# Two modulation blocks multiplied during the router's choice, and the expert buffers in another order

## The chip, the cores and the metric

The kernel runs on one core of one Trainium2 chip. The metric is the device time of one execution in microseconds. All the weights come from the chip's memory in each execution.

## What is computed

Two transformer blocks stand one behind the other, for 256 tokens of width 1024. The change lies in the first one. Cut to what matters:

```
mod = silu(c) @ w_ada + b_ada                 # 1 x 6144: six rows of 1024
sh_m, sc_m, gt_m, sh_f, sc_f, gt_f = split(mod, 6)
h = modulate(rmsnorm(x, g), sh_m, sc_m)
mix = concat(forgetting_attention(h), multiscale_pool(h)) @ w_out
x = x + gt_m * mix
h = modulate(rmsnorm(x, g2), sh_f, sc_f)
lg, le = h @ w_rg + b_rg, h @ w_re + b_re     # router: 4 groups, 8 experts in each
# the best group, in it the best two experts, weights from two softmaxes
y = sum over 32 experts of weight * (silu(h @ w_gate) * (h @ w_up)) @ w_down
x = x + gt_f * y
```

The product for `mod` is made in 12 blocks of 512 columns. Blocks ten and eleven are `gt_f`, the gate by which the experts' sum is multiplied at the end of the block. Nothing before the experts' results needs them. The second block (`second_block` in the reference) has a projection to 5632 columns, two kinds of attention, and an MLP of width 4096.

## The kernel before

**Weights as pieces.** All large weights arrive as pieces of 128 x 2048 numbers (1 MB). SyncE issues them in one fixed order: a list `pieces`, whose entry `i` goes into buffer `ring[slot[i]]`. One transfer is one instruction on SyncE's queue, and SyncE waits and issues strictly in order. Before each issue it waits until the piece that was in the buffer before has been used (`freed`). The first 36 pieces are the weights up to the end of the first block's mixer; the last four of them are the two halves each of modulation blocks ten and eleven. Then come 96 expert pieces from number `E0` on, and from `E1` on the weights of the second block. The experts are worked on in groups of four (`y`): four gate-and-up pieces of the first half, four of the second, and the four down pieces, which come behind the gate-and-up pieces of the next group.

**The buffers of the expert pieces.** Seven are the ring's own (`NR = 7`, `raw0` to `raw6`). The others become free as the mixer ends: `XP` is the memory of x, `GP` that of the gathered tokens, `YP` that of the tile `ym`; eight more are the split weights `whi0`, `wlo0` to `whi3`, `wlo3` (each is the memory of a buffer with a number of 7 or more), and two (`HL`, `HL + 1`) the split activations. `turns` is the order in which the expert pieces take these buffers round by round, `first` the order of the first round, with `GP` and `YP` in it, and `ends` that of the last pieces. `last` holds the seven ring buffers in the order in which the mixer's pieces leave them: `last[0:3]` held block nine's halves and a piece of w_out, `last[3:7]` the four pieces of blocks ten and eleven. In the list before, `first` is XP, GP, last[0:5], whi0, wlo0, last[5:7], whi1, wlo1, YP, whi2, wlo2, whi3, wlo3, HL, HL + 1.

For the three borrowed buffers and the split ones the issuing function `sp_piece` waits for the end of the work that used them:

```
if slot[i] == XP:
    e.wait_ge(*at(("x0", "turned", 3)))
elif slot[i] == GP:
    e.wait_ge(*at(("valued", 3)))
elif slot[i] == YP:
    for n in (("valued", 3), ("mixed", 3), ("ada_rows", 11)):
        e.wait_ge(*at(n))
elif slot[i] >= NR:
    e.wait_ge(*at(("wread", 8 + (slot[i] - NR) % NS if slot[i] < HL else 11)))
```

`wread 8` and `wread 9` come with the first and the second half of the first round of products with w_out (`pe_mix_part(e, n, 1)`, n below 4 and from 4 on), `wread 10` and `wread 11` with those of the second round. `("ada_rows", b)` comes with the last of block b's products. These read `crep`, the activated vector c repeated to 32 columns, and `crep` lies inside the memory that later is `ym`.

**A modulation block.** `pe_block` multiplies its two pieces by `crep` in 8 matmuls of 32 columns of weights and 512 numbers of output (`pe_rows`). ScalarE copies the partial rows to `acc` (`act_ada`). For blocks ten and eleven `pe_ada` adds the partial rows by one more product, and VectorE adds the result to `GTF` (`dve_ada`). Every product here is in full fp32 except those of the split weights; a matmul in fp32 shows in the trace as two instructions.

**The order of the work.** TensorE: first round with w_out for n below 4, block ten, the router's constant row (`shift`), block eleven, first round for n from 4 on, the second round with w_out (n from 0 to 7) with the closing products of both blocks behind n = 1 and the transposes back and the router's logits between; then `pe_moe`. This begins with five dummy products (`pe_awake`), waits for `mask`, makes the rank products (each chosen token's place in its expert), one more dummy, and then gathers the tokens and runs the expert groups. VectorE makes the router's choice meanwhile (`dve_route`), the picking matrices (`dve_pick`), the low halves of the normalised rows (`dve_low_rows`) and the weights. `Banks([...])` gives out banks of PSUM in turn; taking one waits until what was in it has been read.

Of the kernel before, what the change touches and what calls it, by code (L numbers as in the profile page):

```python
# [107 lines left out]
def build(nc, a, out):  # L108
# [3 lines left out]
    with root:  # L112
# [228 lines left out]
        for i in range(NP):  # L341
            if i == E0:
                last = [(taken + k) % NR for k in range(NR)]
                parts_ = [NR + k + NS * h for k in range(NS) for h in range(2)]
                turns = [XP] + last[0:5] + parts_[0:2] + last[5:] + parts_[2:] + [HL, HL + 1]
                first = turns[0:1] + [GP] + turns[1:12] + [YP] + turns[12:]
                ends = [NR, NR + NS] + parts_[2:6] + [(E1 + k) % NR for k in range(NR)] + parts_[6:] + [HL, HL + 1, XP]
            if pieces[i][0] == "exp":
                n = i - E0 - len(first)
                k = first[n] if n < 0 else turns[n % len(turns)] if i < E1 - len(ends) else ends[i - E1 + len(ends)]  # L350
                last_exp[k] = i
            elif i in fixed:
                k = fixed[i]
            else:
                k = (taken if i < E0 else i) % NR
                taken += 1
            earlier.append(in_slot.get(k))
            use.append(1 + slot.count(k))
            slot.append(k)
            in_slot[k] = i  # L360
# [139 lines left out]
        def act_ada(e, b):  # L500
            e.wait_ge(*at(("ada_rows", b)))
            e.wait_ge(*at(("mod", b - 2)))
            e.activation(acc[b % 2][:, :], bank(("ada_rows", b))[:, :], ACT.Copy).then_inc(
                *ada_act(("read", ("ada_rows", b)), ("acc", b)))
# [62 lines left out]
        def dve_ada(e, b):  # L567
            if 6 <= b < 10:
                s = dve_turn_back(e, acc[b % 2], ("ada_rows", b))
                e.tensor_tensor(mcol[:, b // 2, 4 * (b % 2):4 * (b % 2) + 4], s, badc[:, 4 * b:4 * b + 4], ALU.add).then_inc(  # L570
                    *mix_dve(("mod", b)))
                return
            p = bank(("ada", b))
            e.wait_ge(*at(("ada_sum", b)))
            if b >= 10:
                d = GTF[:, 512 * (b % 2):512 * (b % 2) + 512]
                e.wait_ge(*loaded("gtf"))
                e.tensor_tensor(d, d, p[:, :], ALU.add).then_inc(*mix_dve(("read", ("ada", b)), ("mod", b)))
            else:
                d = mcol[:, b // 2, 4 * (b % 2):4 * (b % 2) + 4]  # L580
                e.wait_ge(*loaded("badc"))
                e.tensor_tensor(d, p[:, 0:4], badc[:, 4 * b:4 * b + 4], ALU.add).then_inc(
                    *mix_dve(("read", ("ada", b)), ("mod", b)))
# [189 lines left out]
        def act_mixer(e):  # L773
            e.preload_act_table_set("natural_log_exp_and_others")
            e.wait_ge(*loaded("c"))
            e.activation(ce[:, :], cc[:, :], ACT.Exp, scale=-1.0).then_inc(*mix_act("ce"))
            for t in range(2):
                if t == 0:
                    e.wait_ge(*loaded("first"))
                act_stat(e, t, loaded("x"), mix_act, "n1")  # L780
            act_pieces(e, 3)
            act_high(e, mix_act, "n1", (0,))
            act_pieces(e, 5)
            act_high(e, mix_act, "n1", (1,))
            act_pieces(e, 10)
            act_high(e, mix_act, "n1", (2,))
            act_pieces(e, 13)
            act_high(e, mix_act, "n1", (3,))
            act_pieces(e, 14)
            e.wait_ge(*at("flog_parts"))  # L790
            e.activation(dT[:, 0, :], bank("flog_parts")[:, 0:256], ACT.Copy).then_inc(*mix_act(("read", "flog_parts"), "flog_out"))
            act_copy(e, qT, -0.125, mix_act, "q")
            act_pieces(e, 16)
            e.wait_ge(*at("lt"))
            e.activation(lf[:, :, :], lt[:, :, :], ACT.Abs).then_inc(*mix_act())
            e.wait_ge(*mix_act.last())
            e.activation(lf[:, :, :], lf[:, :, :], ACT.Exp, scale=-1.0).then_inc(*mix_act())
            e.wait_ge(*mix_act.last())
            e.activation(lf[:, :, :], lf[:, :, :], ACT.Ln, bias=1.0).then_inc(*mix_act("lf_log"))
            act_copy(e, kT, 1.0, mix_act, "k")  # L800
            act_pieces(e, 18)
            act_rows(e, vt, 0, mix_act, "v")
            act_soft(e, 0)
            act_soft(e, 1)
            act_rows(e, vt, 1, mix_act, "v")
            act_pieces(e, 21)
            act_soft(e, 2)
            act_soft(e, 3)
            act_rows(e, ut, 0, mix_act, "u")
            act_xt(e, range(2))  # L810
            act_pieces(e, 23)
            act_xt(e, range(2, 4))
            act_soft(e, 4)
            act_soft(e, 5)
            act_rows(e, ut, 1, mix_act, "u")
            act_heads(e, 0)
            act_soft(e, 6)
            act_soft(e, 7)
            act_heads(e, 1)
            for g in range(2):  # L820
                act_band(e, g)
            act_pieces(e, 29)
            for g in range(2, 4):
                act_band(e, g)
            act_heads(e, 2)
            for g in range(2):
                act_pooled(e, g)
            for g in range(2, 4):
                act_pooled(e, g)
            act_pieces(e, 31)  # L830
            act_heads(e, 3)
            act_ada(e, 10)
            act_ada(e, 11)
            act_pieces(e, E0)

        def act_soft(e, h):
# [30 lines left out]
        def dve_mixer(e):  # L867
# [106 lines left out]
            for n in range(8):  # L974
                e.wait_ge(*at(("mix_sum", n)))
                e.wait_ge(*at(("x0", "T", n // 2)))
                e.scalar_tensor_tensor(out=XT[:, n, :], in0=ps[n % 4][:, 256 * (n // 4):256 * (n // 4) + 256],
                                       scalar=mcol[:, 2, n:n + 1], in1=XT[:, n, :], op0=ALU.mult, op1=ALU.add).then_inc(
                    *mix_dve(("x1", n), ("read", ("x1", n))))
                if n == 1:  # L980
                    dve_ada(e, 10)
                    dve_ada(e, 11)

        def dve_scores(e, h):
            p = bank(("sc", h))
# [31 lines left out]
        def pe_mixer(e):  # L1017
# [87 lines left out]
            for n in range(4):  # L1105
                pe_mix_part(e, n, 1)
            rest = Banks([4, 5, 6])
            pe_block(e, rest, 10)
            p = rest.take(e, "shift")
            e.wait_ge(*at(("mod", 7)))  # L1110
            e.wait_ge(*loaded("wr"))
            for c in range(8):
                i = mm(e, p[:, 0:36], BF[:, c:c + 1].broadcast_to([128, 128]), WR[:, c, :], c == 0, c == 7)
            i.then_inc(*mix_pe("shifted"))
            pe_block(e, rest, 11)
            for n in range(4, 8):
                pe_mix_part(e, n, 1)
            for n in range(8):
                pe_mix_part(e, n, 0)
                if n == 1:  # L1120
                    for b in (10, 11):
                        pe_ada(e, Banks([5 + 2 * (b % 2)]), b)
                if n:
                    pe_back(e, n - 1)
                if n == 6:
                    pe_logits(e, 0)
                    pe_logits(e, 1)
# [8 lines left out]
        def pe_block(e, banks, b):  # L1136
            for k in range(2):
                pe_rows(e, banks, b, k)
# [108 lines left out]
        def act_moe(e):  # L1247
# [10 lines left out]
            for h in range(2):  # L1258
                for t in range(2):
                    e.activation(XNH[:, t, 512 * h:512 * h + 512], ps[4 + 2 * t + h][:, :], ACT.Copy, scale=rs[:, t:t + 1]).then_inc(  # L1260
                        *moe_act(("xnh", 2 * t + h)))
            e.wait_ge(*at("lg_less"))
            e.activation(r4[1][:, :, :], r4[1][:, :, :], ACT.Exp).then_inc(*moe_act("lg_exp"))
            for q in range(2):
# [36 lines left out]
        def dve_moe(e):  # L1301
            e.wait_ge(*at(("n2sq", 1)))
            e.tensor_tensor(ss[:, :], ss[:, :], ss2[:, :], ALU.add).then_inc(*rt_dve("ss"))
            dve_route(e)
            dve_pick(e, 0)
            dve_distance(e)
            dve_low_rows(e, 1)
            dve_flag(e)
            dve_weights(e)
            dve_spread(e, 0)  # L1310
# [159 lines left out]
            e.tensor_tensor(OH[0][:, :, :], OH[0][:, :, :], OH[1][:, :, :], ALU.add).then_inc(*step("weights"))  # L1470

        def pe_moe(e, banks):
            pe_awake(e, 5, ("x1", 5))
            p = Banks([3]).take(e, "rank")
            e.wait_ge(*at("mask"))
            mm(e, p[:, 0:32], C["su"], MK[:, 0, :], True, True)
# [1 line left out]
            mm(e, p[:, 32:64], C["su"], MK[:, 1, :], False, True)  # L1478
            mm(e, p[:, 64:96], C["ones"], MK[:, 0, :], True, False)
            mm(e, p[:, 64:96], C["ones"], MK[:, 1, :], False, True).then_inc(*moe_pe("ranked"))  # L1480
            pe_awake(e, 1, ("x1", 5))
            gb, ub, db, tb = Banks([0, 2]), Banks([1]), Banks([2, 0]), Banks([3])
            for q in range(2):
                pe_gather(e, gb, 0, q)
            for y in range(NQ + 1):
# [57 lines left out]
                           ring[slot[i[s]]][:, w], f == 0, f == 1)  # L1543
            x.then_inc(*moe_pe(("down", y, n), *[("freed", i[s]) for s in range(4)] if n else []))


        def pe_awake(e, n, before):
            e.wait_ge(*at(("read", before)))
            e.wait_ge(*loaded("later"))
            for i in range(n):  # L1550
                mm(e, ps[1][:, :], C["ident"], cst[:, NCONST - 512:], True, True)

        def pe_combine(e, y, n):
            e.wait_ge(*at(("WT", y)))
# [1077 lines left out]
```

## Time and profile before

| | us |
|---|---|
| median of 3 runs | 758.48 |
| lowest and highest | 758.19, 758.9 |
| span of the profiled execution | 756.9 |
| TensorE busy in it | 685.3 |
| VectorE busy | 366.3 |
| ScalarE busy | 291.0 |

The profiled execution's own time is its span, from the first instruction to the last. It lies 1.6 us under the median of the runs, which also holds what stands before the first and behind the last instruction. Shares of the whole span say little here, since the kernel has parts with different limits; the rows below are taken from stretches of it. A transfer's row gives when SyncE issued it; its landing is told in a row of its own as the time from the issue.

### The profile page before, as it was taken

The numbers are of one execution on the slowest core, as the hardware profiler recorded it, in microseconds if no ns is written. First come the engines' busy times: TensorE is split into PE (matmuls) and PEld (weight loads), VectorE is DVE, ScalarE is ACT, GpSimd is POOL, SyncE is SP. The second block draws the span as 40 slices with busy tenths as digits, with TensorE's granted clock in tenths as the row PEclk, the third lists the DMA queues.
The fourth block names the chain that finished last, engine by engine and source line by source line (L and its number), as shares of the span: only waits on it lengthen the run. The fifth ranks groups of instructions, "written<-read, shape, count | busy, mean of one in ns | idle before, by whom it ended". The sixth has DMA issues, their size and how long they took to land.

```text
span 756.9 us, 13008 instructions
## 1 busy us (share of the span) xinstructions
PE 685.3 (91%) x5450; PEld 534.3 (71%) x5450; DVE 366.3 (48%) x585; ACT 291.0 (38%) x426; POOL 48.7 (6%) x84
## 2 busy tenths in 40 slices
PE   3999999999767577768999999999999999999996
PEld 2987878843323132213999989999989999998895
DVE  3668861521101010104877987644875744555553
ACT  4345440341110010004666552668456543344532
POOL 0000000000000000000048650000000000000000
PEclk9999999999989898889999999999999999999999
DMA  8999999999999999999944534420655545664001
GB/s 352 405 415 409 358 421 419 421 419 422 424 422 423 424 422 425 397 417 417 374 180 158 215 119 171 159 111 1 223 175 187 197 145 215 223 220 170 1 1 55
DMA packets 33038, 210.27 MB, mean 278 GB/s; under 512 B 4688, under 2 KB 5072, under 8 KB 8656
## 3 DMA queue, kind: packets, MB, share of 16 engines
q1 hardware_dynamic: 32976, 209.38, 69.2%
q8 instruction: 46, 0.75, 0.4%
q14 instruction: 16, 0.13, 0.0%
HBM read 208.32 MB, written 1.05 MB: 277 GB/s over the span
## 4 chain that ended last, share of the span: by engine, by line
PE 71%; DMA 22%; DVE 2%; ACT 2%; SPq 1%; issue 1%; DVEq 0%
PE psum L421 70%; DMA raw<-in_w_exp 17%; DMA raw<-in_w_in_t 3%; PE psum L429 1%; SPq L476 1%; DMA raw<-in_w_in 1%; DMA raw<-in_w_ada_q 1%; ACT whi L497 0%; DVE X L2481 0%; DVE wlo L514 0%; ACT G L1293 0%; ACT XT L2428 0%; DVE gates L2090 0%; DVE dT L1012 0%; ACT MH L1859 0%
## 5 line engine op out<-in xcount | busy, mean ns | idle before, releaser
L421 PE MATMUL psum<-XH,whi 128*128 128x256 f32 x736 | 210.6, 286 | 3.8 <-DVE XL L667 2.5
L421 PE MATMUL psum<-XH,wlo 128*128 128x256 f32 x736 | 208.1, 283 | 0.0
L421 PE MATMUL psum<-XL,whi 128*128 128x256 f32 x736 | 207.8, 282 | 0.0
L514 DVE TENSOR_TENSOR wlo<-raw,whi 128x2048 fp32r<-128x2048 f32 (+1 forms) x88 | 168.7, 1957 | 35.8 <-ACT whi L497 35.8
L497 ACT ACTIVATE whi<-raw 128x2048 fp32r<-128x2048 f32 (+1 forms) x79 | 139.4, 1802 | 55.3 <-PE psum L421 37.1
L421 PEld LDWEIGHTS psum<-XH,whi 128*128 128x128 f32 x736 | 139.0, 189 | 8.5 <-issue 4.0
L421 PEld LDWEIGHTS psum<-XL,whi 128*128 128x128 f32 x736 | 138.7, 188 | 0.3
L421 PEld LDWEIGHTS psum<-XH,wlo 128*128 128x128 f32 x736 | 138.7, 189 | 0.0
L421 PE MATMUL psum<-raw,G 128*32 128x512 f32 x456 | 67.9, 684 | 20.0 <-DMA raw<-in_w_exp 20.0
L421 PEld LDWEIGHTS psum<-raw,G 128*32 128x32 f32 x456 | 17.9, 123 | 57.5 <-issue 56.5
L421 PE MATMUL psum<-raw,XT 128*32 128x512 f32 x248 | 38.0, 749 | 19.7 <-DMA raw<-in_w_exp 18.4
L1277 ACT ACTIVATE WT<-psum 128x256 f32<-128x256 f32 x8 | 3.1, 384 | 133.5 <-PE psum L421 97.6
L421 PE MATMUL psum<-whi,FL 128*128 128x512 f32 (+1 forms) x132 | 50.6, 384 | 0.0
L421 PE MATMUL psum<-wlo,FH 128*128 128x512 f32 (+1 forms) x132 | 50.6, 383 | 0.0
L421 PE MATMUL psum<-whi,FH 128*128 128x512 f32 (+1 forms) x132 | 50.5, 383 | 0.0
L421 PEld LDWEIGHTS psum<-raw,XT 128*32 128x32 f32 x248 | 10.1, 133 | 42.8 <-issue 42.8
L1341 DVE TENSOR_TENSOR ym<-psum,GT 128x512 f32<-128x512 f32 x16 | 11.1, 691 | 59.9 <-PE psum L421 59.9
L1331 DVE TENSOR_TENSOR XT<-XT,psum 128x256 f32<-128x256 f32 x8 | 3.4, 421 | 68.6 <-ACT XT L1282 68.6
L1744 POOL TENSOR_TENSOR XT<-xn 128x128 f32<-128x128 f32 x12 | 9.2, 767 | 392.6 <-DVE xn L2005 389.0
L421 PE MATMUL psum<-ym,WT 128*128 128x512 f32 x64 | 29.1, 595 | 0.9 <-DVE ym L1341 0.9
L2448 DVE TENSOR_TENSOR af<-af,psum 128x512 f32<-128x512 f32 x16 | 11.0, 686 | 38.9 <-ACT af L2407 38.9
L2407 ACT ACTIVATE af<-psum 128x512 f32<-128x512 f32 x16 | 9.6, 600 | 50.1 <-PE psum L421 50.0
(351 smaller groups left out, 947.3 us busy)
## 6 DMA issues: line engine op xcount, KB each, us to landing
raw<-in_w_exp SPq DMA_DIRECT2D x85, 1024.0 KB, 22.9
raw<-in_w_ff SPq DMA_DIRECT2D x32, 1024.0 KB, 5.3
raw<-in_w_in SPq DMA_DIRECT2D x22, 1024.0 KB, 7.3
raw<-in_w_ada SPq DMA_DIRECT2D x16, 1024.0 KB, 11.9
raw<-in_w_in_t SPq DMA_DIRECT2D x8, 1024.0 KB, 18.1
X<-in_w_exp SPq DMA_DIRECT2D x5, 1024.0 KB, 26.5
raw<-in_w_ada_q SPq DMA_DIRECT2D x4, 1024.0 KB, 17.3
raw<-in_w_out_t SPq DMA_DIRECT2D x4, 1024.0 KB, 12.3
```

The source lines that it names most:

```text
L421: return e.matmul(o, l, r, start=start, stop=stop, skip_group_check=True)
L429: return e.transpose(o, x, C["ident"][0:p, 0:p])
L476: e.dma_start(dst, src).then_inc(small[name], 16)
L497: e.activation(whi[j % NS][:, x], ring[slot[i]][:, x], ACT.Copy).then_inc(*hi_made(("hi", j), ("hi", j, x.start // 1024)))
L514: e.tensor_tensor(wlo[j % NS][:, x], ring[slot[i]][:, x], whi[j % NS][:, x], ALU.subtract).then_inc(*steps_(("lo", j, x.start // 1024), *[ ...
L1277: e.activation(WT[y % 2][:, :], bank(("w", y))[:, 0:256], ACT.Copy).then_inc(*moe_act(("read", ("w", y)), ("WT", y)))
L1331: e.tensor_tensor(ac[b], sa[b], bank(("gu", y))[:, 256:512], ALU.mult).then_inc(*moe_dve(("read", ("gu", y)), ("act", y)))
L1341: e.tensor_tensor(ym[:, y % 2, cs], bank(("d", y, n))[:, :], GTF[:, cs], ALU.mult).then_inc(*moe_dve(("read", ("d", y, n)), ("y", y, n)))
L1744: e.tensor_tensor(ev[:, :, 1, :], bv[:, :, 1, :], ref, ALU.subtract).then_inc(*hyb_pool())
L2407: e.activation(af[q][:, :], bank((("ff1", j), q))[:, :], ACT.Relu).then_inc(*ff_act(("relu", j, q)))
L2448: e.tensor_tensor(af[q][:, :], af[q][:, :], bank((("ff1", j), q))[:, :], ALU.mult).then_inc(*ff_dve(("read", (("ff1", j), q)), ("square", ...
```

## The change

Blocks ten and eleven are taken out of the mixer: their products (`pe_block`), their copies (`act_ada`), their closing products (`pe_ada`) and their additions (`dve_ada`). They now stand in the expert part. TensorE does both blocks and their closing products at the start of `pe_moe`, in place of the dummy products, ahead of the rank products. ScalarE's copies follow the first and the second half of XNH. VectorE's additions stand behind `dve_pick(e, 0)` and behind `dve_low_rows(e, 1)`. The gathers take banks 2 and 0 in that order.

The list of the expert buffers changes with it. `first` is now XP, GP, last[0:3], whi0, wlo0, whi1, wlo1, YP, whi2, wlo2, whi3, wlo3, HL, HL + 1, last[3:7]. The condition of `YP` in `sp_piece` is unchanged.

```diff
--- before.py
+++ after.py
@@ -342,8 +342,8 @@
             if i == E0:
                 last = [(taken + k) % NR for k in range(NR)]
                 parts_ = [NR + k + NS * h for k in range(NS) for h in range(2)]
-                turns = [XP] + last[0:5] + parts_[0:2] + last[5:] + parts_[2:] + [HL, HL + 1]
-                first = turns[0:1] + [GP] + turns[1:12] + [YP] + turns[12:]
+                turns = [XP] + last[0:3] + parts_ + [HL, HL + 1] + last[3:]
+                first = turns[0:1] + [GP] + turns[1:8] + [YP] + turns[8:]
                 ends = [NR, NR + NS] + parts_[2:6] + [(E1 + k) % NR for k in range(NR)] + parts_[6:] + [HL, HL + 1, XP]
             if pieces[i][0] == "exp":
                 n = i - E0 - len(first)
@@ -829,8 +829,6 @@
                 act_pooled(e, g)
             act_pieces(e, 31)
             act_heads(e, 3)
-            act_ada(e, 10)
-            act_ada(e, 11)
             act_pieces(e, E0)
 
         def act_soft(e, h):
@@ -977,9 +975,6 @@
                 e.scalar_tensor_tensor(out=XT[:, n, :], in0=ps[n % 4][:, 256 * (n // 4):256 * (n // 4) + 256],
                                        scalar=mcol[:, 2, n:n + 1], in1=XT[:, n, :], op0=ALU.mult, op1=ALU.add).then_inc(
                     *mix_dve(("x1", n), ("read", ("x1", n))))
-                if n == 1:
-                    dve_ada(e, 10)
-                    dve_ada(e, 11)
 
         def dve_scores(e, h):
             p = bank(("sc", h))
@@ -1105,21 +1100,16 @@
             for n in range(4):
                 pe_mix_part(e, n, 1)
             rest = Banks([4, 5, 6])
-            pe_block(e, rest, 10)
             p = rest.take(e, "shift")
             e.wait_ge(*at(("mod", 7)))
             e.wait_ge(*loaded("wr"))
             for c in range(8):
                 i = mm(e, p[:, 0:36], BF[:, c:c + 1].broadcast_to([128, 128]), WR[:, c, :], c == 0, c == 7)
             i.then_inc(*mix_pe("shifted"))
-            pe_block(e, rest, 11)
             for n in range(4, 8):
                 pe_mix_part(e, n, 1)
             for n in range(8):
                 pe_mix_part(e, n, 0)
-                if n == 1:
-                    for b in (10, 11):
-                        pe_ada(e, Banks([5 + 2 * (b % 2)]), b)
                 if n:
                     pe_back(e, n - 1)
                 if n == 6:
@@ -1259,6 +1249,7 @@
                 for t in range(2):
                     e.activation(XNH[:, t, 512 * h:512 * h + 512], ps[4 + 2 * t + h][:, :], ACT.Copy, scale=rs[:, t:t + 1]).then_inc(
                         *moe_act(("xnh", 2 * t + h)))
+                act_ada(e, 10 + h)
             e.wait_ge(*at("lg_less"))
             e.activation(r4[1][:, :, :], r4[1][:, :, :], ACT.Exp).then_inc(*moe_act("lg_exp"))
             for q in range(2):
@@ -1303,8 +1294,10 @@
             e.tensor_tensor(ss[:, :], ss[:, :], ss2[:, :], ALU.add).then_inc(*rt_dve("ss"))
             dve_route(e)
             dve_pick(e, 0)
+            dve_ada(e, 11)
             dve_distance(e)
             dve_low_rows(e, 1)
+            dve_ada(e, 10)
             dve_flag(e)
             dve_weights(e)
             dve_spread(e, 0)
@@ -1470,7 +1463,10 @@
             e.tensor_tensor(OH[0][:, :, :], OH[0][:, :, :], OH[1][:, :, :], ALU.add).then_inc(*step("weights"))
 
         def pe_moe(e, banks):
-            pe_awake(e, 5, ("x1", 5))
+            pe_block(e, Banks([1]), 10)
+            pe_block(e, Banks([2]), 11)
+            pe_ada(e, Banks([1]), 10)
+            pe_ada(e, Banks([0]), 11)
             p = Banks([3]).take(e, "rank")
             e.wait_ge(*at("mask"))
             mm(e, p[:, 0:32], C["su"], MK[:, 0, :], True, True)
@@ -1478,8 +1474,7 @@
             mm(e, p[:, 32:64], C["su"], MK[:, 1, :], False, True)
             mm(e, p[:, 64:96], C["ones"], MK[:, 0, :], True, False)
             mm(e, p[:, 64:96], C["ones"], MK[:, 1, :], False, True).then_inc(*moe_pe("ranked"))
-            pe_awake(e, 1, ("x1", 5))
-            gb, ub, db, tb = Banks([0, 2]), Banks([1]), Banks([2, 0]), Banks([3])
+            gb, ub, db, tb = Banks([2, 0]), Banks([1]), Banks([2, 0]), Banks([3])
             for q in range(2):
                 pe_gather(e, gb, 0, q)
             for y in range(NQ + 1):
@@ -1543,12 +1538,6 @@
                            ring[slot[i[s]]][:, w], f == 0, f == 1)
             x.then_inc(*moe_pe(("down", y, n), *[("freed", i[s]) for s in range(4)] if n else []))
 
-
-        def pe_awake(e, n, before):
-            e.wait_ge(*at(("read", before)))
-            e.wait_ge(*loaded("later"))
-            for i in range(n):
-                mm(e, ps[1][:, :], C["ident"], cst[:, NCONST - 512:], True, True)
 
         def pe_combine(e, y, n):
             e.wait_ge(*at(("WT", y)))
```

## Rows read from the trace of the kernel before

**Rows 1.** The page of the profile: its first line

```profile
span 756.9 us, 13008 instructions
```

**Rows 2.** Stretches: us, busy us (instructions) of each engine, granted clock, DMA share, GB/s

```profile
120.00:150.00 30.00, 29.78 (x212) 25.33 (x211) 11.71 (x41) 5.55 (x15) 0.00 (x0) 1.00 1.01 421
...
220.00:340.00 120.00, 84.60 (x472) 28.56 (x472) 11.21 (x21) 6.65 (x15) 0.00 (x0) 0.83 1.01 418
...
360.00:756.00 396.00, 389.47 (x3088) 358.60 (x3086) 248.23 (x317) 205.15 (x254) 48.56 (x80) 1.00 0.42 157
```

**Rows 3.** TensorE's waits from 150 to 360 us: in total, times, longest

```profile
PE psum L421 <- DMA raw<-in_w_exp: 42.8, 12, 6.3
```

**Rows 4.** Chain of work that ended last, 310 to 440 us: start, us, what

```profile
344.17 9.39 DMA raw<-in_w_in
...
356.86 3.08 PE psum L421 x24
```

**Rows 5.** Timeline of SyncE's issues from 115.5 us: start, us, line, transfer, number

```profile
115.84 7.53 SPq L461 DMA_DIRECT2D raw<-in_w_exp  x4
123.50 0.35 SPq L461 DMA_DIRECT2D ym<-in_w_exp  x1
130.90 10.18 SPq L461 DMA_DIRECT2D raw<-in_w_exp  x6
147.01 0.33 SPq L476 DMA_DIRECT2D GT<-in_norm_final_g  x1
155.64 0.33 SPq L461 DMA_DIRECT2D X<-in_w_exp  x1
```

**Rows 6.** Us to landing of the issues at 115.8, 155.6, 452.6, 454.8, 588.6, 590.8 us

```profile
raw<-in_w_exp SPq DMA_DIRECT2D x1, 1024.0 KB, 17.8
...
X<-in_w_exp SPq DMA_DIRECT2D x1, 1024.0 KB, 6.4
...
raw<-in_w_o_hg SPq DMA_DIRECT2D x1, 1024.0 KB, 4.9
...
raw<-in_w_o_sb SPq DMA_DIRECT2D x1, 1024.0 KB, 6.6
...
raw<-in_w_ff SPq DMA_DIRECT2D x1, 1024.0 KB, 4.8
...
raw<-in_w_ff SPq DMA_DIRECT2D x1, 1024.0 KB, 5.1
```

**Rows 7.** Timeline, 110.8 to 127 us: start, us, engine, line, operation [idle before]

```profile
110.96 1.92 PE L421 MATMUL psum<-raw,crep 128*32 128x512 f32 x16
112.81 1.97 PE L421 MATMUL psum<-GT,mcol 128*128 128x36 f32 x16
...
112.95 0.60 ACT L503 ACTIVATE acc<-psum 128x512 f32<-128x512 f32 x1 [5.26 <-PE psum L421]
...
114.72 1.93 PE L421 MATMUL psum<-raw,crep 128*32 128x512 f32 x16
...
125.22 1.88 PE L421 MATMUL psum<-acc,cst 128*128 128x512 f32 x4
126.94 0.27 PE L421 MATMUL psum<-cst,XT 128*128 128x128 f32 x1
```

**Rows 8.** Timeline of TensorE: dummies, rank products, gate and up of group 2

```profile
142.60 4.54 PE L421 MATMUL psum<-cst 128*128 128x512 f32 x10
...
147.13 1.27 PE L421 MATMUL psum<-MK,cst 128*128 128x32 f32 x10
...
177.94 0.59 PE L421 MATMUL psum<-X,G 128*32 128x512 f32 x1
```

**Rows 9.** Timelines of ScalarE and VectorE: XNH, mask, one addition to GT

```profile
143.16 2.43 ACT L1260 ACTIVATE XNH<-psum,rs 128x512 fp32r<-128x512 f32 x4
...
146.75 0.23 DVE L1395 TENSOR_TENSOR MK<-MK,r 128x64 f32<-128x64 f32 x1
...
126.28 0.69 DVE L578 TENSOR_TENSOR GT<-GT,psum 128x512 f32<-128x512 f32 x1 [0.37 <-PE psum L421]
```

## The prediction

> **What bounds the kernel now.** I read the page first, then the stretches, then TensorE's waits, then SyncE's queue. The page gives the span that the sum is made against [rows 1]; its shares mix two parts, so the stretches must decide. From 120 to 340 us the DMA engines have a share of 1.01 and move 418 to 421 GB/s, while TensorE is busy for only 84.60 of 120 us; from 360 us on the DMA share is 0.42 and TensorE is busy for 389.47 of 396 us [rows 2]. Up to about 355 us the kernel is as long as its weights take to arrive; after that it is as long as TensorE works. The waits agree: between 150 and 360 us TensorE waits 12 times for expert weights, 42.8 us in all [rows 3], and all of that lies behind 192 us. The chain that ended last shows the hand-over: weights of the second block, issued at 344.17, land 9.39 us later, ScalarE and VectorE split them, and from 356.86 us TensorE leads [rows 4].
>
> Two consequences. Time saved on TensorE or VectorE before 355 us is worth nothing by itself: the last expert weight lands when it lands. And an interruption of the DMA stream before 355 us is paid in full, for there is no stretch in which to catch up.
>
> A transfer of 1 MB takes its turn in 2.47 us: the one issued at 115.84 lands 17.8 us later, at 133.6, and the one issued at 155.64 lands 6.4 us later, at 162.0 [rows 5, 6]. Between them lie 10 more expert transfers (three of the four in the first row, ym, six) and `fin`, of half the size [rows 5], so it is 28.4 us for 11.5 turns.
>
> **The code that matters.** SyncE waits and issues in order. I count the expert transfers from 0 (the one into X). Before, position 9 goes into a slot that block eleven's first half frees, and is the one issued at 115.84. The transfer into ym is position 13, issued at 123.50 [rows 5]. One of its conditions is the end of block eleven's products (`("ada_rows", 11)`), because `crep`, which those products read, lies in the same memory as ym. In the kernel before this was met at 116.7 us and cost nothing. The diff does two things at once: it moves block eleven's products to the beginning of `pe_moe`, behind all of the router's logits, and it moves ym from position 13 to position 9. It leaves the condition.
>
> **What is removed ahead of the router.** On TensorE block ten's 16 instructions run from 110.96 to the next group at 112.81 (1.85 us); block eleven's, begun at 114.72, take as long; the two closing products over `acc` run from 125.22 to 126.94 (1.72) [rows 7]. TensorE is busy for 29.78 of the 30 us from 120 to 150 [rows 2], so what stands behind them moves forward by 1.85 + 1.85 + 1.72 = 5.42 us. The two copies on ScalarE and two additions on VectorE lay in idle time there and cost nothing. The dummies begin at 142.60 [rows 8]; in the changed kernel `pe_moe` begins at 142.60 - 5.42 = 137.18.
>
> **What is added in `pe_moe`.** Block ten's products take 137.18 to 139.03, block eleven's to 140.88; they stand where 10 dummy instructions held TensorE for 4.54 us until the mask came [rows 8]. A closing product is 1.72 / 2 = 0.86 us. The first needs ScalarE's copy of 0.60 us [rows 7], behind two of the four copies to XNH (2.43 us for four, from 143.16 - 5.42 = 137.74 on [rows 9]), and has it at 139.8. The second needs a copy that starts when block eleven is done, at 141.0, and ends at 141.6; TensorE is through at about 142.6. The mask is ready at 146.98 - 5.42 = 141.6 [rows 9]. So the rank products start at about 142.7 instead of 147.13 [rows 8]: the choice is 4.4 us earlier, not 5.4. VectorE's two additions (0.69 us each [rows 9]) now stand in the routing chain, and the first expert product needs bank 1 back from the second of them; that takes about 0.7 us more, and 3.7 us are left. By the argument above they are worth nothing.
>
> **What the queue pays.** Positions 5 to 8 now go to whi0, wlo0, whi1, wlo1. The first two are free when the first round of w_out's products is done, at 110.96. The other two wait for the second round, which before began when block eleven ended (116.6) and was over at 115.84 + 7.53 = 123.4 at the latest [rows 5, 7]; it is 3.7 us earlier now. All four are issued by 120 us, and position 8 lands at 133.6 - 2.47 = 131.2 us. Then SyncE stands at ym. What block ten's products let go starts 0.14 us after the next group (the copy at 112.95 against 112.81 [rows 7]), so ym is issued at 140.88 + 0.14 = 141.0 us. From 131.2 us on no weight is in flight. Behind ym wait positions 10 to 19, `fin` and everything after.
>
> What an issue into an empty queue costs is shown later, where the queue does run dry: 4.8 us to landing for the issue at 588.6 and 4.9 for the one at 452.6 [rows 6]. So ym lands at 141.0 + 4.8 = 145.8 us in place of 133.6: 12.2 us. The second of such a pair lands 2.6 us behind the first in one case (590.8 + 5.1 against 588.6 + 4.8) and 3.9 in the other (454.8 + 6.6 against 452.6 + 4.9) [rows 6], against a turn of 2.47: 0.1 to 1.4 us more. I take 0.6, for ten issues 0.4 us apart fill the queue better than the pair, whose issues lie 2.2 us apart. The sum is 12.8 us. Bounds: the fastest restart with no second loss, 12.2 us; the 6.4 us of the issue at 155.64, the row nearest in time, with 1.4, 15.2 us.
>
> The Trainium skill, in "DMA: Bandwidth & Descriptors", section "Anatomy of one DMA", gives a fixed 2.0 us and the bytes at 436 GB/s for the path through GpSimd. For 1 MB that is an estimate of 4.4 us; rows 6 show 4.8 for SyncE's path. With the page's figure the sum would be 12.4 us.
>
> **Why it is not given back.** Until 192 us TensorE waits for no weight, for it is behind the landings, so the first effect is hidden. Positions 20 to 23, used at 177.94 before [rows 8], have landed by 162.0 + 3 x 2.47 = 169.5. Now they land by 182.3, and TensorE, which could be there at 174.2, waits. From there on each wait of [rows 3] comes back 12.8 us later, since each is for a transfer that is 12.8 us later. The new order gives no second gap: in the middle of the stage a slot comes round after 18 transfers in both orders, and the piece with the shortest distance near the end (7 transfers, position 84) waits for the same piece as before. After 355 us TensorE is the bound and starts 12.8 us later.
>
> **The sum.** 0 (work ahead of the router) + 0 (earlier choice) + 12.8 (empty queue) = 12.8 us. The profiled span of 756.9 us [rows 1] becomes 769.7. The median of the runs, 758.48 us, lies 1.6 above it; carried over, that is 771.3 us.
>
> **The rivals.**
> *The choice sets the pace (the other side).* If the expert stage waited for the router, the earlier start would count: -3.7 us, 754.8 us. For it: TensorE has no idle time to speak of up to 150 us [rows 2]. Against it: it waits 42.8 us for weights afterwards [rows 3]. It decides only if ym is issued by 133.6 - 4.8 = 128.8 us; block eleven would have to end 12.2 us sooner than I find. Chance 0.03.
> *The gap is swallowed.* TensorE uses positions 20 to 23 at 177.94 us, 8.4 us after they have landed. Were the stage bound by TensorE from there on, 12.8 - 8.4 - 3.7 = 0.7 us would be left: 759.2 us, no change. The 42.8 us of waits and the full DMA share speak against it. Chance 0.04.
> *The gap costs more.* In it and after it TensorE idles where it was busy, and the granted clock, at a mean of 0.83 between 220 and 340 us already [rows 2], could be low at a worse place. Ten us of products at the lower level that ran at the higher before would, at double the time, be 5 to 10 us; a third of that falling behind the last landing gives 3.4 us: 774.7 us. Chance 0.10.
> *Mine:* 0.83.
>
> **The range.** The likeliest case has 12.2 to 15.2 us from the restart, and the landings of the stage are uneven by about 1 us: 769.7 to 774.7. Widened to 769.0 it takes in a restart somewhat cheaper than my cheapest row, and to 775.0 part of the dearer rival. A run tells about 0.2% (1.5 us) from no change. Slower by more: 0.83 + 0.10 = 0.93; within: 0.04; faster: 0.03.
>
> **What would show it.** In the changed profile: the issue into ym at about 141 us, waiting for TensorE; a DMA share near zero from 131 to 143 us; the rank products at about 142.7; a first wait for an expert weight well before 192 us; those waits at about 42.8 + 12.8 + 3.7 = 59 us in all; TensorE's lead beginning at about 369.7 instead of 356.86. I am wrong if ym is issued before 129 us, if TensorE's waits for weights do not grow, or if the DMA share stays at 1.0.

## The result and the profile after

The changed kernel takes 771.93 us (median of 4 runs, 771.54 to 772.29) against 758.49 (758.19 to 758.9): +13.4 us, ratio 1.0179, 95% interval 1.0166 to 1.0191. The profiled execution has a span of 770.5 us, 13.6 more than [rows 1].

The first thing to look at is SyncE's queue. The timeline of its issues in the changed kernel, to be held against [rows 5]:

```profile
110.06 9.55 SPq L461 DMA_DIRECT2D raw<-in_w_exp  x6
141.00 0.33 SPq L461 DMA_DIRECT2D ym<-in_w_exp  x1
...
147.26 1.91 SPq L476 DMA_DIRECT2D GT<-in_norm_final_g  x1
151.60 0.33 SPq L461 DMA_DIRECT2D X<-in_w_exp  x1
```

Six issues end at 119.61, and then nothing is issued for 21.4 us. SyncE's own waits name what it stood for, TensorE, and that it was one wait:

```profile
SPq L457 <- PE psum L421: 21.3, 1, 21.3
```

Line 457 is the condition of `YP` in `sp_piece`. The times to landing of the issue at 141.00 and of the one at 141.37 behind it:

```profile
ym<-in_w_exp SPq DMA_DIRECT2D x1, 1024.0 KB, 5.0
...
raw<-in_w_exp SPq DMA_DIRECT2D x1, 1024.0 KB, 8.4
```

So ym lands at 146.0 us, where the piece at position 9 landed at 133.6 before [rows 5, 6]: 12.4 us late. The next lands at 149.8, 3.8 us behind it and not 2.47, which is another 1.3 us.

TensorE and the two other engines around the router's choice, to be held against [rows 7 to 9]:

```profile
137.22 3.64 PE L421 MATMUL psum<-raw,crep 128*32 128x512 f32 x32
140.79 1.98 PE L421 MATMUL psum<-acc,cst 128*128 128x512 f32 x4
142.61 1.20 PE L421 MATMUL psum<-MK,cst 128*128 128x32 f32 x10
...
147.90 0.62 PE L421 MATMUL psum<-X,G 128*32 128x512 f32 x1 [0.78 <-DVE GT L578]
...
172.35 5.30 PE L421 MATMUL psum<-raw,XT 128*32 128x512 f32 x32 [2.14 <-DMA raw<-in_w_exp]
183.90 1.03 PE L421 MATMUL psum<-X,G 128*32 128x512 f32 x1 [6.25 <-DMA raw<-in_w_exp]
```

Both blocks' products start at 137.22, the rank products at 142.61 in place of 147.13, and the first expert product at 147.90 in place of 151.95. At 172.35, where TensorE had waited for no weight before, it waits 2.14 us, and at 183.90 it waits 6.25 us for the pieces that it used at 177.94 before [rows 8]. Its waits for expert weights from 150 to 374 us, against [rows 3]:

```profile
PE psum L421 <- DMA raw<-in_w_exp: 54.2, 14, 7.3
```

The stretches, against [rows 2] (us, busy us (instructions) of each engine, granted clock, DMA share, GB/s):

```profile
130.00:145.00 15.00, 13.84 (x112) 10.10 (x110) 7.11 (x30) 5.44 (x13) 0.00 (x0) 1.00 0.21 66
150.00:190.00 40.00, 31.07 (x230) 12.70 (x222) 5.52 (x14) 7.35 (x16) 0.00 (x0) 0.87 1.01 421
...
360.00:372.00 12.00, 11.12 (x61) 4.80 (x54) 6.40 (x10) 5.91 (x13) 0.00 (x0) 0.86 1.03 424
372.00:768.00 396.00, 391.08 (x3101) 360.16 (x3099) 249.70 (x320) 206.30 (x257) 48.59 (x80) 1.00 0.43 156
```

From 130 to 145 us the DMA share is 0.21; it is 1.01 behind that, so nothing is caught up. From 372 us on TensorE is as busy as it was from 360 us on before.

The beginning of TensorE's long stretch of the second block in the chain that ended last, first before and then after:

```profile
360.82 72.91 PE psum L421 x726
```

```profile
374.35 72.90 PE psum L421 x728
```

It is 13.53 us later and as long as it was. The 13.5 us are all made before it. The last expert transfer in the order of issue, into half of X, was issued at 340.01 and landed after 10.8 us before, and was issued at 352.80 and landed after 10.9 now. That is 12.9 us later. In between the delay was first larger than the 12.4 + 1.3 = 13.7 us of the gap. The transfer into x's buffer (position 20), issued at 151.60, landed at 176.2 us:

```profile
X<-in_w_exp SPq DMA_DIRECT2D x1, 1024.0 KB, 24.6
```

That is 14.2 us behind the 162.0 of before [rows 6]; 0.5 us of it came with `fin`, ahead of it in the queue. Then the kernel before had a late landing of its own. These are the landing times of its issues at 179.10 and 179.58:

```profile
raw<-in_w_exp SPq DMA_DIRECT2D x1, 1024.0 KB, 22.6
...
raw<-in_w_exp SPq DMA_DIRECT2D x1, 1024.0 KB, 26.1
```

They landed at 201.7 and 205.7, 4.0 us apart and not 2.5. The changed kernel has no such landing there, so 12.7 us remained, and the rest of the stage added 0.2. At the hand-over to the second block TensorE, at a granted clock of 0.86 where it had 1.00 before, adds some 0.6 us.

### The profile page after: what moved, and what is told of

Read it like the earlier page. It is cut to its first block, busy times and chain, and to the rows that moved or that the text cites. A ratio compares the mean times of both kernels' runs of the same rounds, so it can differ in the third digit from the quotient of the medians.

```text
span 770.5 us, 12982 instructions
## 1 busy us (share of the span) xinstructions
PE 687.0 (89%) x5438; PEld 533.5 (69%) x5438; DVE 366.0 (48%) x585; ACT 290.8 (38%) x426; POOL 48.8 (6%) x84
## 4 chain that ended last, share of the span: by engine, by line
PE 66%; DMA 27%; SPq 2%; DVE 2%; ACT 1%; issue 1%; DVEq 0%
PE psum L421 65%; DMA raw<-in_w_exp 23%; DMA raw<-in_w_in_t 3%; PE psum L429 1%; SPq L476 1%; DMA raw<-in_w_ada_q 1%; SPq L461 1%; DVE X L2470 0%; ACT whi L497 0%; ACT XT L2417 0%; DVE gates L2079 0%; DVE dT L1007 0%; ACT MH L1848 0%; ACT XH L858 0%; DVE wlo L514 0%
## 5 line engine op out<-in xcount | busy, mean ns | idle before, releaser
L421 PEld LDWEIGHTS psum<-XL,whi 128*128 128x128 f32 x736 | 138.6, 188 | 0.3
L421 PE MATMUL psum<-raw,G 128*32 128x512 f32 x456 | 69.5, 691 | 19.4 <-DMA raw<-in_w_exp 19.2
L421 PE MATMUL psum<-raw,XT 128*32 128x512 f32 x248 | 43.6, 841 | 25.9 <-DMA raw<-in_w_exp 25.0
L421 PE MATMUL psum<-X,G 128*32 128x512 f32 x40 | 23.4, 741 | 10.7 <-DMA raw<-in_w_exp 9.9
## 6 DMA issues: line engine op xcount, KB each, us to landing
raw<-in_w_ada SPq DMA_DIRECT2D x16, 1024.0 KB, 11.4
```

The lines of the kernel that those rows point to most:

```text
L421: return e.matmul(o, l, r, start=start, stop=stop, skip_group_check=True)
```

## The experiments

Each kernel was run beside the kernel before on the same chip; "before" below is the median of those runs. Experiments 1, 2 and 4 edit the changed kernel, the others the kernel before.

**1. The wait taken away.** `crep` gets memory that no transfer of the first round takes, so the wait is not needed. The work in `pe_moe` and the order of the buffers stay as in the change.

```diff
-        sb("gap1", [128, 88])
+        crep = sb("crep", [128, 8, 32])
...
-        crep = t1("crep", [128, 8, 32])
+        t1("hole", [128, 8, 32])
...
-                    for n in (("valued", 3), ("mixed", 3), ("ada_rows", 11)):
+                    for n in (("valued", 3), ("mixed", 3)):
```

> The changed kernel, but crep has memory of its own, so that the transfer into ym (still position 9) no longer waits for block eleven's products. Theory (the whole loss is the stream of weights that stands still behind ym): ym is issued at about 119.6 us, the stream never runs dry, and the time is that of the kernel before, 758.5 us (757.5 to 760). Rival (the work put into the routing chain costs): 771 us, as the chain is the same. Rival (the earlier choice counts once the gap is gone): 754.8 us.

761.35 us (before 758.22), ratio 1.0045 (1.0032 to 1.0059). SyncE's issues:

```profile
120.01 0.36 SPq L461 DMA_DIRECT2D ym<-in_w_exp  x1
125.70 15.84 SPq L461 DMA_DIRECT2D raw<-in_w_exp  x10
```

The issue into ym is at 120.01 and the stream runs through: DMA share 1.01 from 120 to 150 us and from 150 to 340. Ten of the 13.4 us are gone. But 3.1 us more than nothing remain, where I had expected at most 1.5. Two rows of the chain say where. The long stretch of the second block begins 1.0 us earlier than before (359.82), so the expert stage is not the place; and its last long piece is longer. This kernel:

```profile
359.82 72.94 PE psum L421 x726
...
571.68 174.87 PE psum L421 x1116
```

The kernel before:

```profile
572.14 172.68 PE psum L421 x1116
```

The same 1116 instructions of the MLP, without a wait in either, take 2.2 us longer. The change has nothing there; my edit has moved all the memory behind `gap1` by (256 - 88) x 4 = 672 bytes. Experiments 2 and 3 part the two.

**2. The wait taken away, and no other memory moved.** The same, but `crep` stands behind `acc`, where nothing of the expert part lies, and `gap1` stays.

```diff
-        crep = t1("crep", [128, 8, 32])
+        t1("hole", [128, 8, 32])
...
         acc = [t1(f"acc{i}", [128, 512]) for i in range(2)]
+        crep = t1("crep", [128, 8, 32])
...
-                    for n in (("valued", 3), ("mixed", 3), ("ada_rows", 11)):
+                    for n in (("valued", 3), ("mixed", 3)):
```

> Like the run with crep in memory of its own, but the memory of nothing else moves: crep stands behind acc, at the end of the mixer's tiles, where no later tile of the expert part lies. In the run before, the stream of weights ran through and TensorE's work on the second block began 1.0 us earlier than in the kernel before (359.82 against 360.82 us), but then took 2.7 us longer. Theory (that remainder came from the memory moved by 672 bytes, and not from the change): 758.5 us, ratio 0.999 to 1.001. Rival (the remainder belongs to the change): 761 us.

758.34 us (before 758.27), ratio 1.0012 (1.0000 to 1.0024): no difference that a run can tell, with a few of its 11 executions 2 to 4 us above the others. Its issues and its chain:

```profile
119.87 0.36 SPq L462 DMA_DIRECT2D ym<-in_w_exp  x1
```

```profile
359.89 72.92 PE psum L422 x726
...
571.23 172.91 PE psum L422 x1116
```

The long piece is back at 172.91 us. The ranks start at 142.75 and the first expert product at 148.05, 4.4 and 3.9 us earlier than before. No dummies stand behind the ranks any more: TensorE idles 1.2 us there, until 145.11, and in the stretch behind that the granted clock is at the lower level for a part.

```profile
145.00:150.00 5.00, 4.83 (x28) 3.14 (x32) 4.09 (x17) 2.97 (x6) 0.00 (x0) 0.66 1.02 424
```

That does not come in each execution: the changed kernel idles as long at this place, and its clock from 145 to 150 us was 1.00 in one trace and 0.66 in that of experiment 8. Here it takes nothing from the time, as little as the earlier start gives. This kernel has the whole of the change but for the wait: the same work in the routing chain, the same order of the buffers, the earlier choice. The wait was the loss, and the earlier choice is worth nothing.

**3. The memory moved and nothing else,** in the kernel before.

```diff
-        sb("gap1", [128, 88])
+        sb("gap1", [128, 256])
```

> The kernel before with nothing changed but the unused gap ahead of the mixer's tiles, which grows from 88 to 256 numbers, so that all the memory behind it moves by 672 bytes, as in the first run with crep in memory of its own. Theory (the move alone makes the second block's products slower): +2.7 us, 761.0 us, with the expert stage unchanged. Rival (that remainder had another cause): 758.3 us.

761.12 us (before 758.47), ratio 1.0032 (1.0020 to 1.0044). One group of the MLP's products, by form, from 572 to 744 us: before, then with the memory moved (number, then busy us, mean ns of one).

```profile
L421 PE MATMUL psum<-wlo,FH 128*128 128x512 f32 x119 | 46.4, 390 | 0.0
```

```profile
L421 PE MATMUL psum<-wlo,FH 128*128 128x512 f32 x116 | 46.2, 399 | 0.0
```

The long piece of the MLP takes as long as in experiment 1, and the second block's stretch begins at 359.94:

```profile
571.77 175.09 PE psum L421 x1116
```

The remainder of experiment 1 is the moved memory's. This kernel has the old choice and begins the second block 0.9 us earlier than the trace before (360.82) all the same, so the 1.0 and 0.9 us in experiments 1 and 2 are no gain of the earlier choice.

**4. ym in other places of the order.** The condition stays, and ym is at position 11, 13 or 19 instead of 9. The edit for 13 (the one for 11 has `[1:10]` and `[10:]`, the one for 19 `turns[1:]` ahead of `[YP]`):

```diff
-                first = turns[0:1] + [GP] + turns[1:8] + [YP] + turns[8:]
+                first = turns[0:1] + [GP] + turns[1:12] + [YP] + turns[12:]
```

> The changed kernel with ym at position 11. Turn 138.6, landing 146.0: 7.4 us late and 1.3 for the second: +8.7 us, 767.2 us. With positions 9, 13 and 19 this is a line of 2.48 us for each position if the theory holds.

> The changed kernel with ym at position 13, where it stood before. It is issued at 141.0 and lands at 146.0, its turn is 143.6: 2.4 us late, and 1.3 for the second behind the gap: +3.7 us, 762.2 us. A rival by which any wait at ym costs the same whatever its place would give 771 to 772; one by which the queue's depth hides it would give 758.5.

> The changed kernel with ym moved from position 9 to position 19, the last of the first round; its condition stays, and it is still issued at 141.0 us at the earliest. Theory: position 19 has its turn at 158.4 us, so the wait costs nothing. Position 11 now is whi3, free at 139.3 - 5.4 = 133.9 us, with its turn at 138.6: 4.7 us, just what an empty queue takes, so 0 to 1.7 us may be lost there: 759.3 us (758.3 to 760.5). Rival (the work in the routing chain costs): 771 us.

| position of ym | expected, us | measured | over before | ratio (95%) |
|---|---|---|---|---|
| 9 (the change) | 771.3 | 771.93 | +13.4 | 1.0179 (1.0166 to 1.0191) |
| 11 | 767.2 | 767.15 | +8.9 | 1.0113 (1.0099 to 1.0128) |
| 13 | 762.2 | 763.17 | +5.0 | 1.0068 (1.0053 to 1.0082) |
| 19 | 759.3 | 760.28 | +2.1 | 1.0022 (1.0013 to 1.0031) |

In all four ym is issued between 140.8 and 142.0 us; what differs is how long the transfers ahead of it keep the stream going. Two positions are worth 4.5 and 4.0 us, against two turns of 4.9. The rival of a fixed price for any wait, and that of a queue deep enough to hide it, are both out. With ym last a loss remains that has nothing to do with ym. Its landing times for the issues at 134.46 (whi3, position 11) and at 135.80 (HL + 1, three issues later):

```profile
raw<-in_w_exp SPq DMA_DIRECT2D x1, 1024.0 KB, 4.9
...
raw<-in_w_exp SPq DMA_DIRECT2D x1, 1024.0 KB, 12.1
```

The first lands at 139.3, some 0.7 us behind the turn worked out for it (138.6). The other lands at 147.9, where three turns behind the first would be 146.7: another 1.2 us. Together they are the upper end of what I had expected, but only the 0.7 us belong to the late buffer. The other transfer took 12.1 us to land, so the queue had work; that it came to the same size is chance. With ym at 13, whi3 (issued at 134.35, 5.1 us to landing) is 0.9 us behind its turn as well, but ahead of the gap at ym, so it is not added: ym, issued at 141.52, landed 4.9 us later, at 146.4, 2.8 us behind its turn, and the next (issued at 141.90, 8.1 us) 3.6 us behind it. Together that is 4.0 us, 762.2 us; the profiled execution took 762.12 and the other three 762.76 to 763.89.

**5. The new order alone,** in the kernel before, with both blocks where they stood in the mixer.

```diff
-                turns = [XP] + last[0:5] + parts_[0:2] + last[5:] + parts_[2:] + [HL, HL + 1]
-                first = turns[0:1] + [GP] + turns[1:12] + [YP] + turns[12:]
+                turns = [XP] + last[0:3] + parts_ + [HL, HL + 1] + last[3:]
+                first = turns[0:1] + [GP] + turns[1:8] + [YP] + turns[8:]
```

> The kernel before with the new order of the buffers alone; both blocks stay in the mixer. ym at position 9 is free at 116.7 us, so it costs nothing. But whi2 and whi3 have moved ahead, to positions 10 and 12, and they are free only at 130.9 and 139.3 us; the turns are 136.1 and 141.1. Theory (every late buffer is paid by the stream): 0 to 1.3 us lost at whi2, and with 4.8 to 6.4 us to landing 3.0 to 4.6 at whi3: 762.5 us (761 to 764). Rival (only the condition on ym matters): 758.5 us.

762.89 us (before 758.6), ratio 1.0053 (1.0037 to 1.0068): +4.3 us. Its issues, and the landing times of those at 139.75 (whi3) and at 140.12:

```profile
123.94 0.35 SPq L461 DMA_DIRECT2D ym<-in_w_exp  x1
131.34 11.15 SPq L461 DMA_DIRECT2D raw<-in_w_exp  x7
```

```profile
raw<-in_w_exp SPq DMA_DIRECT2D x1, 1024.0 KB, 5.0
...
raw<-in_w_exp SPq DMA_DIRECT2D x1, 1024.0 KB, 8.6
```

ym is issued without delay and costs nothing. whi3, issued at 139.75, lands at 144.7 with its turn at 141.1, and the next at 148.7, 4.0 us behind. So the new order needs the earlier end of the mixer; what was missed is ym's condition. The other half alone, both blocks moved and the old order of the buffers kept, was not run; ym at position 13 in experiment 4 comes nearest to it.

**6. The choice later.** In the kernel before, ten dummies ahead of the rank products instead of five.

```diff
-            pe_awake(e, 5, ("x1", 5))
+            pe_awake(e, 10, ("x1", 5))
```

> The kernel before with 5 more dummy products ahead of the rank products: the choice is 4.5 us later. Theory: an earlier choice is worth nothing, but a later one is paid, since the first buffer to come round again (x's, position 20) was issued at 155.64 and landed 6.4 us later just in its turn. Issued at 160.2, with the queue empty from 159.6 on, it lands at 165.0 to 166.6 in place of 162.0: +3.0 to +4.6, and up to 1.3 for the second: 762.5 us (761.3 to 764.3). Rival (there is slack on both sides): 758.5 us.

761.96 us (before 758.6), ratio 1.0039 (1.0026 to 1.0053): +3.4 us. The rank products start at 151.30 and the issue into x's buffer (position 20) is at 159.74 instead of 155.64; its landing and that of the next, issued at 160.11:

```profile
X<-in_w_exp SPq DMA_DIRECT2D x1, 1024.0 KB, 4.9
...
raw<-in_w_exp SPq DMA_DIRECT2D x1, 1024.0 KB, 8.2
```

It lands at 164.6 in place of 162.0, and the next 3.7 us behind. So the kernel before stands at the edge: the choice 4.4 us earlier (experiment 2) is worth nothing, 4.2 us later costs 3.4.

**7. The closing products alone.** In the kernel before, only the closing products and VectorE's additions are moved, as in the change; three dummies stay ahead of them and the one behind the rank products goes.

```diff
-                if n == 1:
-                    for b in (10, 11):
-                        pe_ada(e, Banks([5 + 2 * (b % 2)]), b)
...
-            pe_awake(e, 5, ("x1", 5))
+            pe_awake(e, 3, ("x1", 5))
+            pe_ada(e, Banks([1]), 10)
+            pe_ada(e, Banks([0]), 11)
```

> The kernel before with the closing products and the additions on VectorE alone moved behind the router's logits, as in the change; the blocks' products and the order of the buffers stay. The choice comes about 1.7 us earlier. Theory: no weight comes earlier, 758.5 us within 0.2%. Rival (the choice sets the pace): 756.8 us.

758.59 us (before 758.6), ratio 0.9999 (0.9989 to 1.0008). The rank products start at 146.38, only 0.75 us earlier than before. That is not the moved part's doing. Block ten's products stand ahead of everything that was moved, and they already start 0.97 us later than in the trace before (110.96):

```profile
111.93 1.92 PE L421 MATMUL psum<-raw,crep 128*32 128x512 f32 x16
```

Counted from them the rank products come 1.7 us earlier, as expected. So the moved products cost nothing, and a choice 1.7 us earlier gives nothing. The larger step, 4.4 us, is experiment 2's.

**8. The changed kernel again,** beside experiment 2.

> The changed kernel once more, on the same chip as the run beside it, for its landings: 771.9 us; a 12.3 us late landing of ym, some 1.3 us more for the transfer behind it.

773.04 us (before 758.27), ratio 1.0191 (1.0175 to 1.0206), 1.1 us above the first measurement. The issue into ym is at 141.22; it landed after 4.8 us, and the next, issued at 141.59, after 8.2: 3.7 us behind it. The last expert transfer was issued at 352.80 and landed after 10.8 us, as in the other trace of this kernel. The two traces part behind that. The same 20 instructions of the end of the expert part, first in the other trace, then in this one:

```profile
363.80 3.81 PE psum L421 x20
```

```profile
363.35 5.74 PE psum L421 x20
...
375.83 72.95 PE psum L421 x727
```

The second block's long stretch begins 1.5 us later than at 374.35, and the granted clock from 360 to 372 us is 0.72 in place of 0.86. The kernel is the same, and so are its waits there, to 0.2 us.

No version here beats the kernel before. The best is that of experiment 2, with the same time. What the change saves is time of TensorE ahead of an expert stage that is as long as its transfers.

## Why the prediction was right

**The bound.** It named the stream of weights up to 355 us and TensorE behind that. The share of 0.21 at the gap, 1.01 behind it, and TensorE's unchanged second stretch show it.

**The work ahead of the router.** 5.42 us were forecast, and the blocks' products began at 137.22 against 137.18. The ranks began at 142.61 against 142.7, the first expert product at 147.90 against 151.95 - 3.7 = 148.2. The copies and additions did cost what was said: the 0.78 us ahead of the product at 147.90 are its wait for bank 1, which VectorE's second addition (DVE GT L578) gives back.

**The queue.** ym was issued at 141.00, as forecast. The restart took 5.0 us and not 4.8. The term that was mis-sized is that for the second transfer: 0.6 us was taken between 0.1 and 1.4, and it was 1.3. I argued that ten issues 0.4 us apart would fill the queue better than a pair 2.2 us apart. They did not: with ym at 11, with the order alone and with the choice late the transfer behind the restart landed 3.7, 4.0 and 3.7 us after it, always near the dear end. The gap so came to 13.7 us, 0.9 more than the sum had.

**Not given back.** The delay at the last expert transfer was 12.9 us and at the second block 13.5. TensorE's waits for weights grew by 11.4 us and not by the 12.8 + 3.7 = 16.5 that I had written. The missing part is not a gain: with more waits between them, products ran at a lower granted clock. The 32 down products at 172.35, behind a wait of 2.14 us, took 5.30 us. Before, they had taken 3.64:

```profile
174.51 3.64 PE L421 MATMUL psum<-raw,XT 128*32 128x512 f32 x32 [0.25 <-ACT G L1293]
```

The mean from 150 to 190 us was 0.87 where TensorE had been at 1.00 before. The engine was slower in time that it would have waited. The Trainium skill, in "TensorE: Matmul & The Clock Gate", Part 1, says that the clock goes between 1.2 and 2.4 GHz with the engine's activity; that agrees with the row. At the hand-over the time was not free. There the second block began 13.5 us later than before with a clock of 0.86, and 15.0 with 0.72 in the second trace of the same kernel (experiment 8), for a delay of the last weights of 12.9 and 12.8 us. So the lower clock cost some 0.6 us in the one and 2.2 in the other. For the first of the two this rests on the comparison with the kernel before; the 1.5 us between them are shown by the same kernel.

**The rivals.** "The choice sets the pace" is refuted by experiment 2: without the wait the choice is 4 us earlier and the time the same. "The gap is swallowed" is refuted by the landings. "The gap costs more" came true by 0.6 us of its 3.4 in the first trace and by 2.2 in the second. The uneven landings, which I had put at 1 us either way, came to 0.8 in the kernel's favour: 0.5 against it at `fin` and 0.2 in the rest of the stage, and 1.5 for it, because the trace before has its late landing at 205.7. Most of the other traces show such delays of 0.3 to 1.5 us too, at this or other places and with work enough in the queue; where they come from is open.

**How much of it was luck.** That the sum met the measured time within 0.6 us is partly chance. The gap was 0.9 us dearer than forecast, `fin` and the rest 0.7, and the clock 0.6, and the late landing in the trace before took 1.5 back. The mechanism and the place of the loss are not chance: the issue at 141.0, the empty queue and ym's landing 12.4 us late (12.2 forecast) came as worked out, and experiment 2 takes the whole loss away with the wait.

## What to carry to other kernels

When the queue that feeds a stage waits and issues in order, a transfer's place in the order is a promise that its buffer is free by then: write for each the time when its buffer is free and its turn less the time of a restart, and look at the difference before the work that frees it is moved. A piece of work moved to where an engine has time can be the last reader of memory that someone else waits for; follow its inputs (here `crep`), not only its result. And a stage that is as long as its transfers gives nothing for an earlier start, but takes from a later one at once if the first buffer that comes round again has no reserve.

## What was not expected

A transfer of 1 MB into an empty queue landed after 4.8 to 5.0 us wherever the stream had run dry (ym in both traces of the change and at 11 and 13, whi3 with the order alone, x's buffer with the choice late), but the one issued 0.4 us behind it landed 3.6 to 4.0 us later and not 2.47. Each time the stream of weights ran dry it therefore cost 1.2 to 1.5 us above the late landing of the first transfer. From the third on the spacing was 2.5 us again.

`fin`, of half the size, landed 1.7 us behind the piece ahead of it in the change and 1.2 us behind it before. In the six traces in which a buffer came late ahead of it (the change twice, ym at 11, at 13 and last, the order alone) it took 1.6 to 1.9 us, and in the six others 1.1 to 1.3. Why is not shown.

Moving all tiles by 672 bytes made the MLP's products of 128 x 512 slower, 399 ns instead of 390 for one group, and the kernel 2.65 us longer, with the same instructions, a granted clock of 1.00 in both and no wait in that stretch. Why is not shown: which tile's place it is was not tried. Whoever tests an edit that changes the memory should keep all other addresses, or run the move alone beside it.
